# Two float32r parts in place of three bf16 parts in the expert loop of a two-layer mixture-of-experts trunk

## What is computed

```python
scores = sigmoid(x @ w_router)                      # 256 x 64
idx    = top 8 experts of a token, out of the 4 best of 8 groups
gates  = scores[idx] / sum(scores[idx]) * 2.5
for e in range(64):                                 # SwiGLU, width 256
    y = (silu(x_e @ w_gate[e]) * (x_e @ w_up[e])) @ w_down[e]
    out[tokens of e] += gate * y
out += shared SwiGLU expert on all tokens
x = layer_norm(alpha * x + out)
```

## Time and profile before

| | us |
|---|---|
| median of 3 runs | 1492.9 (1488.49 to 1494.56) |
| the profiled execution, its own time | 1491.75 |
| its span, first to last instruction | 1490.0 |
| TensorE busy | 1433.5 (96%) |
| VectorE, ScalarE, GpSimd busy | 430.7, 341.9, 204.8 |
| DMA, share of 16 engines | 76% |

### The profile page before, as it was taken

How to read it: one execution, slowest core, us unless ns; L and a number is a source line. 1 busy time by engine, 2 the same in 40 slices (tenths; PEclk the granted TensorE clock), 3 DMA queues, 4 the chain that set the end, 5 groups by cost and what they waited for, 6 DMA issues and landing times.

```text
span 1490.0 us, 27151 instructions
## 1 busy us (share of the span) xinstructions
PE 1433.5 (96%) x11324; PEld 811.0 (54%) x11324; DVE 430.7 (29%) x943; ACT 341.9 (23%) x653; POOL 204.8 (14%) x234
## 2 busy tenths in 40 slices
PE   8989999999999999969999998999999999999996
PEld 7868444444444444435697997854444544445442
DVE  2245122221222222163452325622221222212224
ACT  1231222222222222212231433022222222222221
POOL 7100111111111111111001300001111111111111
PEclk9999999999999999989898998999999999999999
DMA  4685899999999999725243005459999999999990
GB/s 153 177 328 213 334 398 407 405 411 401 400 406 408 405 404 399 292 86 177 75 132 133 4 4 228 198 224 402 401 408 407 407 407 393 408 407 408 405 392 29
DMA packets 114301, 449.84 MB, mean 302 GB/s; under 512 B 15648, under 2 KB 44960, under 8 KB 80960
## 3 DMA queue, kind: packets, MB, share of 16 engines
q1 hardware_dynamic: 114240, 448.94, 76.1%
HBM read 447.86 MB, written 1.05 MB: 301 GB/s over the span
## 4 chain that ended last, share of the span: by engine, by line
PE 94%; DVE 2%; ACT 2%; DMA 1%; issue 0%; POOL 0%; POOLq 0%; ACTq 0%; PEldq 0%; DVEq 0%
PE PS L1587 30%; PE PS L1613 15%; PE PS L1621 11%; PE PS L1567 9%; PE PS L451 4%; PE PS L402 3%; PE PS L418 3%; PE PS L1688 2%; PE PS L435 2%; PE PS L1264 1%; PE PS L1283 1%; PE PS L1249 1%; PE PS L1279 1%; PE PS L1171 1%; PE PS L440 1%; PE PS L1593 1%
## 5 line engine op out<-in xcount | busy, mean ns | idle before, releaser
L2089 POOL TENSOR_TENSOR AR<-AR 128x512 bf16<-128x512 f32 x128 | 136.7, 1090 | 901.7 <-ACT AR L1819 901.7
L1587 PE MATMUL PS<-RING,AR 128*64 128x512 f32 x1024 | 225.3, 592 | 1.9 <-issue 1.9
L1587 PE MATMUL PS<-AR 128*64 128x512 f32 x1024 | 225.2, 592 | 0.0
L1621 PE MATMUL PS<-AR 128*128 128x512 bf16 x744 | 181.3, 379 | 0.0
L1899 DVE TENSOR_TENSOR AR<-PS,AR 128x512 f32<-128x512 f32 x128 | 88.6, 692 | 238.6 <-ACT AR L1815 238.6
L1587 PEld LDWEIGHTS PS<-RING,AR 128*64 128x64 f32 x1024 | 74.1, 137 | 146.5 <-issue 146.5
L1587 PEld LDWEIGHTS PS<-AR 128*64 128x64 f32 x1024 | 73.4, 137 | 146.3 <-issue 146.3
L1876 DVE SCALAR_TENSOR_TENSOR AR<-AR,PS 128x256 f32<-128x256 f32 x64 | 30.8, 481 | 381.1 <-ACT AR L1793 381.1
L1567 PE MATMUL PS<-AR 128*128 128x192 bf16 x1024 | 132.2, 245 | 0.0
L1567 PE MATMUL PS<-AR,X 128*128 128x192 bf16 x512 | 125.8, 246 | 0.0
L1621 PEld LDWEIGHTS PS<-AR 128*128 128x128 bf16 x744 | 62.6, 97 | 109.5 <-issue 50.3
(11 more groups left out here) (269 smaller groups left out, 1411.5 us busy)
## 6 DMA issues: line engine op xcount, KB each, us to landing
RING<-in_moe_w_gate SPq DMA_DIRECT2D x64, 1024.0 KB, 8.7
RING<-in_moe_w_up SPq DMA_DIRECT2D x64, 1024.0 KB, 10.8
RING<-in_moe_w_down SPq DMA_DIRECT2D x64, 1024.0 KB, 10.3
AR<-in_moe_w_gate SPq DMA_DIRECT2D x64, 1024.0 KB, 9.4
AR<-in_moe_w_up SPq DMA_DIRECT2D x64, 1024.0 KB, 11.8
AR<-in_moe_w_down SPq DMA_DIRECT2D x64, 1024.0 KB, 8.0
AR<-in_ab_w_in SPq DMA_DIRECT2D x8, 1024.0 KB, 5.6
AR<-in_rw_w_k SPq DMA_DIRECT2D x4, 1024.0 KB, 7.6
```

The lines of the kernel that those rows point to most:

```text
L1587: ins = nc.tensor.matmul(PS[s * B:(s + 1) * B, 4, :], XG[:, k, c:c + B], gate_and_up(slots[s])[:, k, :, :], start=(k == 0), stop=(k == KT ...
L1621: ins = nc.tensor.matmul(PS[:, 2 * t + h, :], OHT[:, half, t, :], YS[:, n, h * 512:(h + 1) * 512], start=(opens and t == 1 and n == 0), st ...
L2089: nc.gpsimd.tensor_tensor(YS[:, 2, c], YR[:, c], YS[:, 1, c], ALU.subtract).then_inc(q[f"low{h}"], 1)
```

## The change

- x is split into two float32r parts, `XH` (x converted) and `XL` (x minus that), in buffers of their own; both are made on GpSimd, each tile when its layer norm is done. VectorE splits nothing any more.
- The gather has 2 parts in place of 3: 32 matmuls for a quad. Its map is a float32r one, `SELR`, with 48 columns per expert. The bf16 map `SEL1` stays for `turn_map`; VectorE now makes both.
- The expert outputs `YS` are two float32r parts: the high part by ScalarE, the low part by VectorE in the place of the rest. The middle part (ScalarE) and the low part on GpSimd are gone. `OHT` is float32r, and the scatter has 4 matmuls per half in place of 6.
- The arena grows from 25000 to 25300 words per partition and gets a fixed place; the routing's scratch lies over the later buffers `XG`, `SIL`, `HH` and `HT`, so the clearing of the unused slots waits for the routing's mask.

```diff
-        XL = am(TT, D)
-        XLO = am(TT * D // 2).bitcast(BF16).rearrange("p (t d) -> p t d", t=TT)
-        XH = X[:, :, :].bitcast(BF16)[:, :, 1::2]
-        XM_ = XL.bitcast(BF16)[:, :, 1::2]
-        XP = [XH, XM_, XLO]
+        XH = split_parts("x_high", am.at, TT, D)
+        XL = split_parts("x_low", am.at + TT * D, TT, D)
+        YS = split_parts("y_parts", am.at + 2 * TT * D, 2, D)
+        OHT = split_parts("token_map", am.at + 2 * TT * D + 2 * D, 2, TT, P)
+        SELR = split_parts("slot_map", am.at + 2 * TT * D + 2 * D + 2 * TT * P, TT, 4, CAP)
+        XP = [XH, XL]
...
+        def split_parts(name, at, *shape):
+
+            return nc.alloc_sbuf_tensor_at(name, [P, *shape], F32R, offset=AR_BASE + 4 * at)
...
-        def split_x(v, link, t):
-
-            link(nc.vector.tensor_tensor(XL[:, t, :], X[:, t, :], XH[:, t, :], ALU.subtract))
+        def split_x(g, link, st, t):
+
+            g.wait_ge(s_ln, TT * st + t + 1)
+            link(nc.gpsimd.tensor_copy(XH[:, t, :], X[:, t, :]))
             link.sync()
-            nc.vector.tensor_tensor(XLO[:, t, :], XL[:, t, :], XM_[:, t, :], ALU.subtract).then_inc(moe_shared["x_split"], 1)
+            nc.gpsimd.tensor_tensor(XL[:, t, :], X[:, t, :], XH[:, t, :], ALU.subtract).then_inc(moe_shared["x_split"], 1)
...
-                        for n in range(3):
+                        for n in range(2):
                             ins = nc.tensor.matmul(PS[:, 7 - part % 2, k * 4 * CAP:(k + 1) * 4 * CAP],
-                                                   XP[n][:, t, 2 * part + k::KT], SEL1[:, t, :, 0:CAP],
-                                                   start=(t == 0 and n == 0), stop=(t == TT - 1 and n == 2))
+                                                   XP[n][:, t, 2 * part + k::KT],
+                                                   SELR[:, t, :, :].rearrange("p s b -> p (s b)"),
+                                                   start=(t == 0 and n == 0), stop=(t == TT - 1 and n == 1))
...
             def scatter(pe, half, h, opens=False):
                 for t in range(TT):
-                    for n in range(3):
+                    for n in range(2):
...
-                for h in range(2):
-                    c = slice(h * 512, (h + 1) * 512)
-                    s.wait_ge(q[f"rest{h}"], i + 1 + past[f"rest{h}"])
-                    nc.scalar.copy(YS[:, 1, c], YR[:, c]).then_inc(q[f"middle{h}"], 1)
...
+                nc.vector.tensor_tensor(SELR[:, :, 0:count, :], spread[:, :, :, 0:CAP], io[:, :, :, 0:CAP], ALU.is_equal)
                 nc.vector.tensor_tensor(SEL1[:, :, 0:count, :], spread, io, ALU.is_equal).then_inc(sem_, 1)
...
-                    nc.vector.tensor_tensor(YR[:, h * 512:(h + 1) * 512], PS[:, 5 + h, :], YS[:, 0, h * 512:(h + 1) * 512],
-                                            ALU.subtract).then_inc(q[f"rest{h}"], 1)
+                    nc.vector.tensor_tensor(YS[:, 1, h * 512:(h + 1) * 512], PS[:, 5 + h, :],
+                                            YS[:, 0, h * 512:(h + 1) * 512], ALU.subtract).then_inc(q[f"low{h}"], 1)
...
-                g.wait_ge(s_ln, TT * st)
+                if l == 0:
+                    g.wait_ge(s_o, 2)
+                for t in range(TT):
+                    split_x(g, L[0], 2 * l, t)
+                g.wait_ge(q["mask_ready"], 1 + past["mask_ready"])
                 nc.gpsimd.memset(XGS[:, :, :, CAP:B], 0.0).then_inc(q["pads_cleared"], 1)
-                with g.Fori(0, PAIRS) as i:
-                    for h in range(2):
-                        c = slice(h * 512, (h + 1) * 512)
-                        g.wait_ge(q[f"middle{h}"], i + 1 + past[f"middle{h}"])
-                        nc.gpsimd.tensor_tensor(YS[:, 2, c], YR[:, c], YS[:, 1, c], ALU.subtract).then_inc(q[f"low{h}"], 1)
```

More of the change, by code:

```diff
@@ L50 @@
 BF16 = mybir.dt.bfloat16
+F32R = mybir.dt.float32r
 ALU = mybir.AluOpType
@@ L119, in program @@
         cnti = sb("cnti", [1, 4], I32)
-        AFL = 25000
-        AR = sb("AR", [P, AFL])
+        AFL = 25300
         PS = ctx.enter_context(nc.psum_tensor("PS", [P, 8, 512], F32))
+        AR_BASE = -(-nc.sbuf_base // 64) * 64
+        AR = nc.alloc_sbuf_tensor_at("AR", [P, AFL], F32, offset=AR_BASE)
+        def split_parts(name, at, *shape):
+            return nc.alloc_sbuf_tensor_at(name, [P, *shape], F32R, offset=AR_BASE + 4 * at)
         class Area:
@@ L148, in wslot @@
                     w[:, 4096:6144].rearrange("p (k f) -> p k f", k=FT))
[L150 to L161, removed]
         gsum = am(TT)
@@ L165, in program @@
         HS = am(FT, T)
-        XL = am(TT, D)
-        XLO = am(TT * D // 2).bitcast(BF16).rearrange("p (t d) -> p t d", t=TT)
-        XH = X[:, :, :].bitcast(BF16)[:, :, 1::2]
-        XM_ = XL.bitcast(BF16)[:, :, 1::2]
-        XP = [XH, XM_, XLO]
+        am.at = -(-am.at // 16) * 16
+        XH = split_parts("x_high", am.at, TT, D)
[3 more added lines that the diff above has]
+        SELR = split_parts("slot_map", am.at + 2 * TT * D + 2 * D + 2 * TT * P, TT, 4, CAP)
+        am.at += 2 * TT * D + 2 * D + 2 * TT * P + TT * 4 * CAP
+        XP = [XH, XL]
         XR_AT = am.at
-        XR = am(TT * D)
+        XR = am(D)
         SEL1 = am(2 * TT * B).bitcast(BF16).rearrange("p (t s b) -> p t s b", t=TT, s=4)
+        XG_AT = am.at
         XG = am(KT, 4 * B)
         XGS = XG.rearrange("p k (s b) -> p k s b", s=4)
+        in_xg = Area(AR, XG_AT, am.at)
+        BIA = in_xg(TT, E)
+        top2 = in_xg(TT * NG, 8)
+        grp = in_xg(TT, NG)
+        cmpa = in_xg(TT, NG, NG)
+        cmpb = in_xg(TT, NG, NG)
+        gcnt = in_xg(TT, NG)
+        gpen = in_xg(TT, NG)
+        REP = in_xg(TT, E)
+        top8 = in_xg(TT, 8)
+        HID_AT = am.at
         SIL = am(FF)
@@ L178, in program @@
         HT = am(FT, 2 * B)
[L179 to L182, removed]
+        in_hid = Area(AR, HID_AT, am.at)
+        SCO = in_hid(TT, E)
+        MSK = in_hid(TT, E)
+        SEL = in_hid(TT, E)
+        GR = in_hid(TT, E)
+        HSs = XR[:, 0:FT * T].rearrange("p (f t) -> p f t", f=FT)
         G3 = am(TT * (E + NOV) * 3 // 2).bitcast(BF16).rearrange("p (t e n) -> p t e n", t=TT, n=3)
         GQ = am(TT * 4 * 3 // 2).bitcast(BF16).rearrange("p (t e n) -> p t e n", t=TT, n=3)
-        GR = am(TT, E)
         GC = am(2)
         F1 = am(3, NR)
-        in_xr = Area(AR, XR_AT + D, XR_AT + D + FT * T)
+        in_xr = Area(AR, XR_AT, XR_AT + FT * T)
         OH = in_xr(NR, NOV)
         OS = in_xr(2, NOV)
-        TR4 = XR[:, D + FT * T:D + FT * T + 4 * P].rearrange("p (m t) -> p m t", m=4)
+        TR4 = XR[:, FT * T:FT * T + 4 * P].rearrange("p (m t) -> p m t", m=4)
         F2 = am(E)
@@ L345, in layer_norm @@
                                                op0=ALU.mult, op1=ALU.add).then_inc(s_ln, 1)
[L346 to L350, removed]
         def act_ln(s, st):
@@ L1485, in program @@
         by_pair = ["gate_up_done", "silu_ready", "hidden_ready", "turned", "hidden_copied", "map_copied", "gates_ready",
-                   "down0", "down1", "high0", "high1", "rest0", "rest1", "middle0", "middle1", "low0", "low1", "scattered"]
+                   "down0", "down1", "high0", "high1", "low0", "low1", "scattered"]
         by_quad = ["onehot_ready"] + [f"gathered{n}" for n in range(4)] + [f"gathered{n}_copied" for n in range(4)]
@@ L1575, in gather_two @@
                     for t in range(TT):
-                        for n in range(3):
+                        for n in range(2):
                             ins = nc.tensor.matmul(PS[:, 6 + half, k * 2 * CAP:(k + 1) * 2 * CAP],
-                                                   XP[n][:, t, 4 * half + k::KT], SEL1[:, t, 0:2, 0:CAP],
-                                                   start=(t == 0 and n == 0), stop=(t == TT - 1 and n == 2))
+                                                   XP[n][:, t, 4 * half + k::KT],
+                                                   SELR[:, t, 0:2, :].rearrange("p s b -> p (s b)"),
+                                                   start=(t == 0 and n == 0), stop=(t == TT - 1 and n == 1))
                 return ins
@@ L1730, in pe_moe @@
                 most = nc.tensor.value_load(cnti[0:1, 2 * l:2 * l + 1], min_val=0, max_val=T)
-                for n, made in enumerate(("high", "middle", "low")):
+                for n, made in enumerate(("high", "low")):
                     for h in range(2):
@@ L1970, in dve_moe @@
                 copy_turned(v, nc.vector.tensor_copy, st, 2)
-                v.wait_ge(s_ln, TT * st)
-                split_x(v, link, 1)
                 dve_route(v, link)
@@ L1993, in dve_moe @@
                     dve_over(v, Link(v, q["over_link"]))
-            OVER_STEPS = 12
+            OVER_STEPS = 8
             def dve_over(v, link):
@@ L2070, in dve_over @@
                         link.sync()
[L2071 to L2075, removed]
```

(1 more changed line is left out.)

## The result

The change makes the kernel slower: 1614.9 us (median of 4 runs, 1611.76 to 1622.87) against 1490.7 us before (median of 4), a ratio of 1.084 with a 95% interval of 1.079 to 1.090. The forecast was 1447 us, faster. The profiled execution has a span of 1610.0 us against 1490.0: 120 us more.

What follows compares the result with a forecast made beforehand. TensorE was taken as the bound, with transfers almost a second one. Per layer 21 us from the loop plus 2 at its end, 46 for two layers, off 1491.75 gives 1445.7, with the median's 1.2 more 1447 us; range 1424 to 1495.

Steps and rivals of the forecast that it cites:

- the price of a gather matmul: Gather: 0.109 us per float32r matmul against 0.086 for bf16; with two parts for three, 0.6 us saved per quad.
- the bounds 0.086 to 0.33: Gather matmul price in us: lower end today's bf16 matmul, upper end ordinary f32 at 192 columns.
- A clock loss I don't count: TensorE in the loops: granted clock stays at 1.00 (2.4 GHz), as coming waits are about 1 us in a quad of 30.
- Rival 2: Gather: 192 columns pay the f32 price, 0.33 us per matmul, while the scatter runs in one pass; 1663 us, chance 0.12.
- Rivals 1 and 3: Gather matmul at 0.16 us, 1488 us, chance 0.07; or half rate in gather and scatter, 1580 us, chance 0.05.
- rival 3: Half rate everywhere: gather matmul 0.165 us, scatter matmul 0.43 us; 1580 us, chance 0.05.
- Rival 4: Gather and scatter: float32r runs as f32 in four passes, 15 us more per quad; 1967 us, chance 0.03.
- Scatter: Four matmuls per half for six, still 0.218 us each: 0.5 us saved per pair, 15.5 us per layer.
- the wait for the gated hidden rows: Behind the scatter's first half, transposes wait for VectorE, so only 0.17 us of that half's 0.44 is saved.
- The end of a layer: Last scatter matmuls no longer wait for GpSimd's low part and go 2.0 us earlier: 2 us per layer.
- all of TensorE's gain: Expert loops: the whole 25 us per layer saved on TensorE counts, where the forecast took 21 because of transfers; 1439 us.
- the lead of 10.6 us: Weight loads land that far ahead of their first reader; usable once per layer when quads outrun the transfers.

## Why the prediction was wrong

**The step that failed: the price of a gather matmul.** The prediction took 0.109 us from the strided f32 transposes, "the nearest row", and named what it shared with the gather: element size, stride, one record. It did not share the mode: a transpose is not a product. The rows with f32 products all load neighbouring elements, and the one row with a strided four-byte load was a transpose; no row had both a stride and a product, and the bounds 0.086 to 0.33 said so. The measured 0.240 lies between them. The term was to be a gain of 0.6 us per quad and is a loss of 7.71 - 4.15 = 3.6. One sign stood in the trace of before: the load records of the strided transposes (L313) are 48 ns longer than those of transposes with neighbouring elements (L619), at the same distance of 0.109. The stride showed there in the record and not in the distance.

```profile
L313 PEld LDWEIGHTS PS<-ident,X x64: 185/189/226, 6.0 to 955.7; 128*128 128x128 f32 x64
L619 PEld LDWEIGHTS PS<-ident,AR x32: 138/141/143, 73.6 to 99.3; 128*128 128x128 f32 x32
```

**The second step: "A clock loss I don't count".** It rested on how little TensorE would wait. It waits nowhere in the quads; it loads. The record of the granted clock falls to 1.2 GHz near the end of the slow gather or just behind it, and that costs 1.3 us per quad and stretches the first gate and up products of a layer too (9.78 us in place of 7.09 at the head of layer 0).

```profile
148.25 9.78 PE L1595 MATMUL PS<-RING,AR 128*64 128x512 f32 x32 [0.94 <-issue]
```

In numbers per quad: gather +3.6, scatter -0.9, clock +1.3, together +3.9 as measured (35.0 against 31.1). Over 15.5 quads in each of two layers that is 121 us, and the span is 120 us longer. The rest (the slow start of each layer, the shorter end, the mixers) then about cancels; it was not broken down.

**The rivals.** Rival 2 had the side right and the point from which it decides (0.161 per gather matmul). Its mechanism, few moving columns, is refuted by the run with 256 columns, and its price of 0.33 is too high: 1663 against 1615. With 0.240 in its sum, which has no clock loss, it comes to about 1570, where the runs with the slow load and a full clock lie (1567.0 and 1569.5). Rivals 1 and 3 assumed a price per column; the column count changes nothing at 0.24, and the scatter's 0.23 is not rival 3's 0.43. Rival 4 is refuted: float32r runs in one record, with 0.11 per matmul where the layout is good, f32 in two.

**The places where the Trainium skill was weighed.** From the Trainium skill, page "FP8 and Floating Point Precision", section "TensorE Precision Notes", where only true FP32 is given four passes, the prediction concluded that float32r takes one. That conclusion holds: the scatter's starts are 0.23 apart with 512 columns. The Trainium skill, page "TensorE: Matmul & The Clock Gate", section "LDWEIGHTS (loading the stationary operand)", gives columns divided by 1.2 GHz, by which 128 take 107 ns (an estimate). The trace agrees for loads of neighbouring elements at the higher clock (0.111) and disagrees at the lower clock (0.214) and for a stride of 4 or 8 four-byte elements (0.235 and 0.240), where the measurement decides. The Trainium skill, page "TensorE: Matmul & The Clock Gate", section "Weight-path perf modes", keeps the fast weight load from FP32, and the prediction feared the same for float32r. The runs fit that, with 0.111 per gather matmul where bf16 has 0.086, but it is not what made the kernel slow.

**What held.**
- Scatter: 0.5 us saved per pair was forecast, 13.53 - 13.06 = 0.47 measured. Its matmuls are 0.23 apart, not 0.218, and the wait for the gated hidden rows that I looked for does not show.
- The end of a layer: in the row of the last rest, 1592.95 + 0.69 = 1593.64, and the layer norm begins at 1594.83, 1.2 us later; before, the rest ended at 1471.24 + 0.69 = 1471.93 and the layer norm began at 1474.81, 2.9 us later. 1.7 us gained per layer, 2.0 forecast.

```profile
1592.95 0.69 DVE L1904 TENSOR_TENSOR y_parts<-PS,y_parts 128x512 fp32r<-128x512 f32 x1 [1.03 <-ACT y_parts L1823]
...
1594.83 1.29 DVE L339 SCALAR_TENSOR_TENSOR X<-X,PS 128x512 f32<-128x512 f32 x2 [1.19 <-PEq L1749]
```

- GpSimd's split of tile 1 is done at 126.35, long before the first gather:

```profile
122.88 1.04 POOL L330 CAST x_high<-X 128x1024 fp32r<-128x1024 f32 x1 [12.40 <-DVE X L355]
124.00 2.35 POOL L332 TENSOR_TENSOR x_low<-X,x_high 128x1024 fp32r<-128x1024 f32 x1
```

- The sum itself: with side by side loads, where a gather matmul costs 0.111, close to the 0.109 that was assumed, the kernel takes 1439.6 us; 1447 was forecast, 1439 with all of TensorE's gain let through. That the last two agree is in part luck: the sum starts from 1492.9, while the kernel before took 1488.4 in the rounds of this run, so the gain is 49 us where the forecast had 46 and the whole of TensorE's gain 54. Still the transfers held nothing back. Their rate was set too low: windows of this kernel show

```profile
312.00:342.00 30.00, 30.00 (x160) 14.08 (x158) 7.37 (x17) 4.83 (x10) 0.00 (x0) 1.00 1.02 418
342.00:372.00 30.00, 30.00 (x160) 14.09 (x158) 7.37 (x17) 4.83 (x10) 0.00 (x0) 1.00 1.02 417
372.00:402.00 30.00, 30.00 (x160) 14.05 (x158) 7.37 (x17) 4.83 (x10) 0.00 (x0) 1.00 1.02 419
```

The engines move 418 GB/s where the 415 and 410 of the earlier trace rows were taken for the limit. A quad needs 12.58 MB / 418 = 30.1 us and takes 29.7; if the lead of 10.6 us pays 0.4 for each of 15 quads, that is 6 us (an estimate), so it lasts to the end of the layer. No wait for a weight transfer shows in the loops.

## What to carry to other kernels

Price a matmul's load from a row with the same element size, the same stride and the same mode; a transpose is not evidence for a product. Before four-byte data (f32 or float32r) becomes the stationary operand, lay it out so that the elements of one load lie side by side, or at most 2 apart: here the layout alone is worth 175 us, and the engine that writes the copy can do it for nothing (GpSimd takes 1.5 us longer for a tile and is still done 11 us before the first gather). And when a change makes loads the limit of a stretch, look at the granted clock behind it, since an engine that is "busy" can lose it.

## What the runs showed of the hardware

- A load of 128 columns of four-byte elements for a product costs 0.111 us at stride 1, 0.119 at 2, 0.235 at 4 and 0.240 at 8 (float32r). For f32 it costs 0.240 at stride 8 and about 0.11 at stride 1 (where 64 and 128 columns cost the same). A transpose costs 0.109 at stride 8. The bf16 gather reads two of its three parts at the same distance of 32 bytes and costs 0.086 per matmul, close to the 0.080 of its 192 columns at 2.4 GHz (an estimate). Why the step lies between 2 and 4 elements, and why transposes and bf16 are spared, no run here tells.
- The slow load keeps its 0.24 when the granted clock is halved, when the DMA engines are idle, and when the columns grow from 192 to 256. A load of neighbouring elements goes from 0.111 to 0.214 at the lower clock.
- The granted clock fell in or behind gathers with 192 columns in one record each 0.24 us, and did not with 256 columns, nor with plain f32. More columns in the same time made the kernel faster by 48 us.
